# Gate row multiplied into the sublayer's sums ahead of the root, and the down tiles of the 64-slot passes fetched as pairs of neighbouring rows

## The reference

```python
def rms_norm(x, g):
    y = x * rsqrt(mean(x * x, -1) + EPS)
    return y * g

for i in range(2):
    sh_a, sc_a, g_a, sh_f, sc_f, g_f = split(silu(c) @ mod_w[i] + mod_b[i], 6)
    y = mixer[i](modulate(x, norm_g[i, 0], sh_a, sc_a))
    x = x + g_a * rms_norm(y, norm_g[i, 1])
    y = channel_mixer[i](modulate(x, norm_g[i, 2], sh_f, sc_f))
    x = x + g_f * rms_norm(y, norm_g[i, 3])

def swiglu(h, w_gate, w_up, w_down):
    return (silu(h @ w_gate) * (h @ w_up)) @ w_down     # w_gate, w_up: 1024 x 3584, w_down: 3584 x 1024
```

## Time and profile before

| | |
|---|---|
| median of 3 runs | 1727.36 us (1723.87 to 1729.08) |
| the profiled execution's own time | 1724.3 us |
| its span, first to last instruction | 1722.6 us |
| PE busy | 1635.9 us (95%) |
| DVE, ACT busy | 893.0 us (52%), 684.7 us (40%) |
| DMA, mean over the span | 293 GB/s |
| mean granted TensorE clock | 0.98 |

### The profile page before, as it was taken

One profiled execution on the slowest core, in us unless ns is written; L12 is line 12 of the kernel. 1 busy time (PEld: TensorE's weight loads), 2 busy tenths in 40 slices (PEclk: granted clock), 3 DMA queues, 4 the chain that ended last, 5 costly groups with the idle time before them and its releaser, 6 DMA issues.

```text
span 1722.6 us, 23953 instructions
## 1 busy us (share of the span) xinstructions
PE 1635.9 (95%) x9497; PEld 1178.1 (68%) x9497; DVE 893.0 (52%) x977; ACT 684.7 (40%) x811; POOL 50.4 (3%) x100
## 2 busy tenths in 40 slices
PE   5999999999999999987899999999999999899997
PEld 4999999789999976732454545545555545788785
DVE  5666766667766679411122222233323214888886
ACT  2444455553333357410221322222232304668674
POOL 0200000001100000000000000000000000000000
PEclk9999999999999999979999999999999999999999
DMA  9986666248887632059999999999999999998993
GB/s 345 343 258 212 204 205 220 94 141 303 300 287 266 230 112 99 25 192 395 368 380 370 382 370 374 367 388 370 381 359 370 378 375 390 358 355 303 377 355 124
DMA packets 245601, 504.78 MB, mean 293 GB/s; under 512 B 11360, under 2 KB 83200, under 8 KB 245504
## 3 DMA queue, kind: packets, MB, share of 16 engines
q1 hardware_dynamic: 230224, 458.26, 73.5%
q0 software_dynamic: 12032, 43.00, 7.0%
q10 hardware_dynamic: 3248, 2.17, 0.4%
HBM read 502.34 MB, written 1.05 MB: 292 GB/s over the span
## 4 chain that ended last, share of the span: by engine, by line
PE 80%; DMA 10%; DVE 5%; ACT 3%; issue 1%; SPq 0%; ACTq 0%; DVEq 0%
PE ps L1513 14%; PE ps L1564 12%; PE ps L1114 10%; PE ps L1118 9%; PE ps L1121 9%; PE ps L1517 8%; DMA raw<-l_exp_w_up 5%; PE ps L1577 4%; DMA raw<-l_exp_w_gate 2%; PE ps L1495 2%; ACT whi L694 1%; PE ps L1685 1%; DMA raw<-l_exp_w_down 1%; PE ps L1169 1%; DVE wlo L1870 1%
## 5 line engine op out<-in xcount | busy, mean ns | idle before, releaser
L1870 DVE TENSOR_TENSOR wlo<-raw,whi 128x2048 fp32r<-128x2048 f32 x218 | 495.9, 2289 | 263.6 <-ACT whi L694 258.8
L694 ACT ACTIVATE whi<-raw 128x2048 fp32r<-128x2048 f32 x218 | 415.1, 1911 | 183.4 <-PE ps L1118 82.0
L1564 PE MATMUL ps<-raw,arena 128*64 128x512 f32 x1120 | 262.6, 612 | 19.9 <-DMA raw<-l_exp_w_up 17.7
L1114 PE MATMUL ps<-ahi,whi 128*128 128x256 f32 x832 | 239.7, 288 | 1.7 <-DVE alo L1938 1.7
L1118 PE MATMUL ps<-alo,whi 128*128 128x256 f32 x832 | 237.0, 285 | 0.0
L1121 PE MATMUL ps<-ahi,wlo 128*128 128x256 f32 x832 | 236.7, 285 | 0.0
L1564 PEld LDWEIGHTS ps<-raw,arena 128*64 128x64 f32 x1120 | 78.6, 140 | 172.8 <-issue 168.4
L1114 PEld LDWEIGHTS ps<-ahi,whi 128*128 128x128 f32 x832 | 161.1, 194 | 5.1 <-issue 3.8
L1118 PEld LDWEIGHTS ps<-alo,whi 128*128 128x128 f32 x832 | 161.1, 194 | 0.3
L1121 PEld LDWEIGHTS ps<-ahi,wlo 128*128 128x128 f32 x832 | 161.2, 194 | 0.0
L1513 PE MATMUL ps<-whi,alo 128*128 128x512 f32 x448 | 160.1, 399 | 0.0
(11 more groups left out here) (275 smaller groups left out, 2113.4 us busy)
## 6 DMA issues: line engine op xcount, KB each, us to landing
raw<-l_exp_w_gate SPq DMA_DIRECT2D x112, 1024.0 KB, 7.9
raw<-l_exp_w_up SPq DMA_DIRECT2D x112, 1024.0 KB, 9.5
raw<-l_exp_w_down SPq DMA_DIRECT2D x112, 1024.0 KB, 10.0
raw<-l_w_in SPq DMA_DIRECT2D x42, 1024.0 KB, 6.3
mraw<-mod_w POOLq DMA_DIRECT2D x80, 512.0 KB, 5.3
raw<-l_ffn_w_gate SPq DMA_DIRECT2D x14, 1024.0 KB, 5.1
raw<-l_ffn_w_up SPq DMA_DIRECT2D x14, 1024.0 KB, 6.9
raw<-l_ffn_w_down SPq DMA_DIRECT2D x14, 1024.0 KB, 6.9
```

Source lines behind the costliest of these rows:

```text
L694: act.activation(whi[n % SPL][:, :], raw[s % RAW][:, :], ACT.Copy).then_inc(hi_done, 1)
L1114: pe.matmul(dst, stat[0], mov[0], start=start, stop=False, skip_group_check=True)
L1564: ins = pe.matmul(half_bank(1, half), slots_of(q)[:, kc, :], raw[(s + half) % RAW][:, kk * BANK:kk * BANK + BANK], start=kc == 0, stop=kc ...
L1870: dve.tensor_tensor(wlo[n % SPL][:, :], raw[s % RAW][:, :], whi[n % SPL][:, :].bitcast(F32), ALU.subtract).then_inc(lo_done, 1)
```

## The change

1. At the ends of sublayers 0 to 2, ACT squares each PSUM bank (512 columns) by itself into scrap (`dg`) with its own sum. DVE adds eps to the first bank's sum (`ss_first`), and the root takes that as its bias. Ahead of the root DVE multiplies each bank by `gb` into `xo`, the first when ACT has squared it, the second when ACT has squared that one. After the reciprocal one operation makes `xs = xo * rstd + xs`.
2. At the last end `yacc * gb` is made ahead of the reciprocal in the same way, in one piece of 1024 columns, and ACT squares it in one piece, as before, into `dg`.
3. The down tiles of the five S passes (70 tiles) are fetched so that partition p holds rows 2p and 2p + 1 of a tile's 256 rows, where it held rows p and 128 + p. `beside_T` turns every second column of a half of `sb_g`, so that `sb_h` fits. Down tiles of other passes stay.

```diff
-            def e_down_static(e, i, s):
+            def e_down_static(e, i, s, pairs):
                 for k in range(2):
-                    fetch(s + k, 0, dram["l1_exp_w_down"][bass.ds(e, 1), i * 512 + 256 * k:i * 512 + 256 * k + 256, :]
-                          .rearrange("a (k p) c -> p (a k) c", p=P), (2, D))
+                    src = dram["l1_exp_w_down"][bass.ds(e, 1), i * 512 + 256 * k:i * 512 + 256 * k + 256, :]
+                    fetch(s + k, 0, src.rearrange("a (p k) c -> p (a k) c" if pairs else "a (k p) c -> p (a k) c", p=P), (2, D))
...
             def squares_out(c, sub, used):
-                squares(c, [ps[:, 2 * tt * BANK:2 * (tt + 1) * BANK] for tt in range(NT)],
-                        [(first_out, sub + 1), (w_used, used)])
+                act.activation(warm[:, :], ones[:, 0:1], ACT.Sqrt)
+                for tt, out_done in enumerate(((first_out, sub + 1), (w_used, used))):
+                    act.wait_ge(*out_done)
+                    for n in range(2):
+                        act.activation(dg[:, n * BANK:(n + 1) * BANK], bank(2 * tt + n), ACT.Square, scale=float(D) ** -0.5,
+                                       accum_out=ss_halves[:, sub, tt, n:n + 1]).then_inc(sq_done if n else half_squared, 1)
+                    act.wait_ge(sq_done, 2 * c + tt + 1)
+                    act.wait_ge(ss_first_done, 2 * sub + tt + 1)
+                    act.activation(rms[:, c, tt:tt + 1], ss_halves[:, sub, tt, 1:2], ACT.Sqrt,
+                                   bias=ss_first[:, sub, tt:tt + 1]).then_inc(sqrt_done, 1)
...
                 for fc in range(4):
-                    ins = pe.transpose(bank(7, fc * P, fc * P + P), sb_g[:, fc * P:fc * P + P], ident)
+                    every_second = sb_g[:, fc // 2 * 256:fc // 2 * 256 + 256].rearrange("p (c k) -> p k c", k=2)[:, fc % 2, :]
+                    ins = pe.transpose(bank(7, fc * P, fc * P + P), every_second, ident)
...
-            def residual(c, sub, ys):
+            def add_residual(c, sub, tt):
+                root(c, tt)
+                dve.wait_ge(post_t, 2 * sub + tt + 1)
+                dve.scalar_tensor_tensor(xs[:, tt, :], xo[:, tt, :], rstd[:, c, tt:tt + 1], xs[:, tt, :], ALU.mult,
+                                         ALU.add).then_inc(x_new, 1)
+            def residual(c, sub):
                 dve.wait_ge(gb_done, sub + 1)
                 if sub == 0:
                     dve.wait_ge(x_ordered, ORDERED)
                 for tt in range(NT):
-                    root(c, tt)
-                    dve.scalar_tensor_tensor(xo[:, tt, :], ys[tt], rstd[:, c, tt:tt + 1], gb[:, :], ALU.mult,
-                                             ALU.mult).then_inc(post_t, 1)
-                    dve.wait_ge(post_t, 2 * sub + tt + 1)
-                    dve.tensor_tensor(xs[:, tt, :], xs[:, tt, :], xo[:, tt, :], ALU.add).then_inc(x_new, 1)
+                    dve.wait_ge(half_squared, 2 * sub + tt + 1)
+                    dve.tensor_tensor(ss_first[:, sub, tt:tt + 1], ss_halves[:, sub, tt, 0:1], eps[:, 0:1],
+                                      ALU.add).then_inc(ss_first_done, 1)
+                    dve.tensor_tensor(xo[:, tt, 0:BANK], bank(2 * tt), gb[:, 0:BANK], ALU.mult)
+                    dve.wait_ge(sq_done, 2 * c + tt + 1)
+                    dve.tensor_tensor(xo[:, tt, BANK:D], bank(2 * tt + 1), gb[:, BANK:D], ALU.mult).then_inc(post_t, 1)
+                    add_residual(c, sub, tt)
```

More of the change, by code:

```diff
@@ L253, in build @@
         rms = sb("rms", [P, 8, NT])
+        ss_halves = sb("ss_halves", [P, 3, NT, 2])
+        ss_first = sb("ss_first", [P, 3, NT])
         rstd = sb("rstd", [P, 8, NT])
@@ L379, in build @@
         sqrt_done = sem("sqrt_done")
+        half_squared = sem("half_squared")
+        ss_first_done = sem("ss_first_done")
         hroot = sem("hroot")
@@ L635, in _ @@
                         u, k = small_before(q, i)
-                        e_down_static(chosen[u], k, s + 4)
+                        e_down_static(chosen[u], k, s + 4, True)
                 elif kind == "G":
@@ L641, in _ @@
                 elif kind == "D":
-                    e_down_static(chosen[q], i, s)
+                    e_down_static(chosen[q], i, s, False)
                 else:
@@ L645, in _ @@
                     e_up(chosen[q], i, s + 2, 0)
-                    e_down_static(chosen[FIRST_M - 1], NF - 1, s + 4)
+                    e_down_static(chosen[FIRST_M - 1], NF - 1, s + 4, True)
             e_gate(chosen[FIRST_M], 1, tile_of(FIRST_M, 1), 0)
@@ L694, in high, with squares @@
                 act.activation(whi[n % SPL][:, :], raw[s % RAW][:, :], ACT.Copy).then_inc(hi_done, 1)
-            def squares(c, srcs, wait_for=None):
+            def squares(c, srcs, wait_for=None, out=lambda tt: xo[:, tt, :]):
                 act.activation(warm[:, :], ones[:, 0:1], ACT.Sqrt)
@@ L702, in squares @@
                         act.wait_ge(*wait_for[tt])
-                    act.activation(xo[:, tt, :], srcs[tt], ACT.Square, scale=float(D) ** -0.5,
+                    act.activation(out(tt), srcs[tt], ACT.Square, scale=float(D) ** -0.5,
                                    accum_out=ss[:, c, tt:tt + 1]).then_inc(sq_done, 1)
@@ L1100, in _ @@
             squares(7, [yacc[:, tt, :] for tt in range(NT)],
-                    [(y_add, 4 * (FIRST_M + loops) - 1), (y_add, 4 * (FIRST_M + loops) + 1)])
+                    [(y_add, 4 * (FIRST_M + loops) - 1), (y_add, 4 * (FIRST_M + loops) + 1)], lambda tt: dg)
             for c in (1, 3):
@@ L2044, in mixer_out @@
                     low(m + j + SPL)
-                residual(c, sub, y_banks)
+                residual(c, sub)
             modulation(1)
@@ L2091, in _ @@
             modulation(2)
-            residual(3, 1, y_banks)
+            residual(3, 1)
             normalise(4, 2)
@@ L2546, in _ @@
                 add_scattered(FIRST_M + 1, tt, 2 + 2 * tt, loops)
-            residual(7, 3, [yacc[:, tt, :] for tt in range(NT)])
+            dve.wait_ge(gb_done, 4)
+            for tt in range(NT):
+                dve.wait_ge(y_add, 4 * (FIRST_M + loops) - 1 + 2 * tt)
+                dve.tensor_tensor(xo[:, tt, :], yacc[:, tt, :], gb[:, :], ALU.mult).then_inc(post_t, 1)
+                add_residual(7, 3, tt)
 _INS = ["x", "c", "mod_w", "mod_b", "norm_g", "l0_w_in", "l0_w_out", "l0_ffn_w_gate", "l0_ffn_w_up", "l0_ffn_w_down",
```

1 line of the change is left out of this document (removed).

## The result

| | before | after |
|---|---|---|
| median | 1725.98 us (8 runs, 1722.09 to 1733.06) | 1717.54 us (8 runs, 1711.34 to 1724.77) |
| the profiled execution's own time | 1724.3 us | 1718.1 us |
| its span | 1722.6 us | 1716.4 us |

The ratio is 0.9948, 95% interval 0.9925 to 0.9971: 0.5% faster. The forecast was 1723.2 us (1716.5 to 1731.0), so the time lies near the lower end of the range, and "within 0.3%", which I held the likeliest, did not come.

A forecast was written before the change was run, and what follows sets the result against it. It took transfers to bound the first expert pass, PE most of the rest, and latency chains the sublayer ends. Ends 1.9, down tiles 2.3 and transposes 0 made 4.2 us off the median 1727.36: 1723.2 us, range 1716.5 to 1731.

The forecast's parts named there:

- within 0.3%: Whole kernel: the time stays the same within 0.3% (5.2 us), about what a measurement can tell; chance 0.53.
- The ends, 1.9 us: Sublayer ends: 0.53 us gained at each of the first three and 0.34 at the last, 1.9 together (0 to 3.0).
- The down tiles, 2.3 us: Expert stage: fewer, larger packets save 0.11 us a tile, 1.4 in the first pass and 0.9 beyond (0 to 7.7).
- the first pass counts whole, 1.4 us: First expert pass, 108 us: bound by transfers, so the saving on all its 13 down tiles shortens the kernel by 1.4 us.
- pay nothing: Down tiles: no gain, as packets are cut at 4 KB or PE is the bound; 1725.5 us, chance 0.20.
- the down tiles pay in full: Expert stage: PE and DMA run so close that all 7.7 us count, with 1.9 from the ends: 1717.8 us, chance 0.16.
- The transposes, 0: `beside_T` in the expert steps: loading every second column changes nothing; bounds 0 and 0.5 us a step.
- a load of 141 ns does not show in a spacing of 125: `beside_T`: loads of 141 ns overlap, four transposes taking 0.50 us, so the strided load was taken to cost 0.
- loads grow: `beside_T`: weight loads of the transposes longer than 141 ns would show the forecast wrong.
- the slower case: Expert steps: half-rate strided loads stall PE 0.5 us a step in about 20 of 35 steps; 1733.2 us, chance 0.12.
- The clock, chance 0.07: After sublayer end 1: shorter PE gaps keep the clock at 2.4 GHz, 3.3 us more gained; 1719.9 us, chance 0.07.
- faster: Whole kernel: faster by more than the 0.3% (5.2 us) a measurement can tell; chance 0.35.

The follow-up runs named there:

- e12: The change with old down tiles and contiguous transposes, and fewer PE fill-in products at ends 0 to 2 (15 in place of 20): 0.9946 of the kernel before.
- e2_pairs: The kernel before with only the new down tiles and transposes, the ends as before: 1727.97 us, 1.0014 of the kernel before.
- e13: The change with old down tiles and contiguous transposes, without any PE fill-in products at ends 0 to 2: 1725.32 us, 1.0001 of the kernel before.
- e9: The kernel before plus one unused tile of 96 bytes per partition, moving later tiles to multiples of 64: 1723.23 us, 0.9985 of the kernel before.
- e10: The change with old down tiles and contiguous transposes, plus a 32-byte spare tile putting hhi and later tiles back at 32 past 64: 0.9996 of before.
- e14_ends_again: A word-for-word repeat of the change with old down tiles and contiguous transposes: 1715.53 us, 0.9938 of the kernel before.
- e3: The whole change again, the same program, run beside its parts on one chip: 1717.95 us, 0.9949 of the kernel before.

## Why the prediction was right in its range and wrong in its reasons

- **The ends, 1.9 us: right in mechanism, small in size.** 2.1 to 2.3 us by the rows. The filler stood ahead of the transposes as worked out (8.01 for 8.02), and e12 shows it from the other side. Mis-sized: the small addition by 0.11 and the last DVE operation by 0.05, and the gain of each end, taken at the transposes' start (0.53) where the next row on DVE shows 0.70 (0.52 at end 1 by the other count).
- **The down tiles, 2.3 us: wrong.** The packets fell by 8960 and the time for each tile by about 0.07 us, but the failed step is "the first pass counts whole, 1.4 us": it gave 0.1 to 0.4, and nothing beyond it can be told from zero. The reading behind it was wrong as well. The prediction took all 108 us of the first pass as landings and so had 130 - 108 = 22 us left beyond it, but its chain has 63 us of landings there. With the transposes the edit most likely costs about 2 us. Rival "pay nothing" was nearest. That the time came out at 1717.5, beside the 1717.8 of "the down tiles pay in full", is chance: e2_pairs, at 1.0014, refutes that rival.
- **The transposes, 0: wrong.** The failed step is "a load of 141 ns does not show in a spacing of 125"; the load did not stay at 141, and that loads grow was one of the signs that the prediction named for being wrong. It costs some 0.085 us a step, inside the bounds (0 and 0.5), not enough for the slower case (0.12 for each transpose).
- **The clock, chance 0.07: underrated.** About 3 us of the gain come with a mean clock of 0.981 in place of 0.979. The mechanism that the rival named, what PE did before, is borne out by e13 for a large change of it. Why new ends and shift together raise it and neither alone does, stays open: neither e9 (0.9780) nor e10 (0.9789) shows a rise, and a profile is one execution.
- **Missing: the shift**, about 4 us. No term and no rival had it, so "faster" got 0.35 only, and a forecast of 4.2 us with two of its three terms wrong ended up within range by luck.

In sum for the change, against 8.4 to 8.7 measured: ends 2.3, shift 4, clock 3, pairs and strided loads -1 to -2. The first is read from rows, the second from rows and from three kernels, the clock's by the straight line; that the clock is a cause of its own here, and not only a companion, is argued and not shown.

The best version is the change without the pairs: e1_ends and e14_ends_again, 13 runs with a mean of 1714.9 us, at 0.9928 and 0.9938. That it beats the change (1716.7 over the 16 runs of after and e3) lies at the edge of what these runs tell; that it beats before is clear of the noise.

## What to carry to other kernels

Before costing an edit, look whether it allocates anything: a small tile moves all tiles behind it, and a kernel compared with its predecessor must be compared at equal addresses, with a spare tile if need be. Of the two positions tried here for the `F32R` operands that PE loads, a multiple of 64 bytes was the faster one; it is worth a trial elsewhere. A cheaper transfer pays only where a landing ends the wait, and a layout that makes it cheaper must not be paid for on the engine that is the bound. And filler in front of waiting work is measured with the clock it buys, never by its own delay alone.

## What the runs showed of the hardware

- In the dense stage, products whose stationary tile (`F32R`) started 32 bytes past a multiple of 64 took 392 to 398 ns, at a multiple of 64 390 to 393 (before, e10_shifted_back; after, e9_aligned); their weight loads read the same in all four (188 ns).
- A float32 weight load of every second column took 209 ns, a contiguous one 141; four transposes took some 0.085 us longer.
- 128 packets of 8 KB in place of 256 of 4 KB moved 0.9% more in one 47 us stretch, some 0.07 us a down tile, which is at the edge of what one execution tells; 512 of 2 KB cost 0.14 us a tile in that stretch, and 2.9 us over the first pass.
- Over 209 runs, 0.001 less mean clock went with 1.45 us more. Without filler the mean clock was 0.972 for 0.981, and the kernel 11 us slower.
